# Hybrid stage: V and dt in one product, the relative bias added by VectorE, the decay sums spread by DMA

## The reference, cut to what matters

```python
h = rms_norm(x, mix_norm); proj = h @ w_in             # z 1024 | xbc 1536 | dt 16 | q 512 | k 512 | v 512
xbc = silu(causal_depthwise_conv(xbc, conv_w, conv_b)) # 4 taps; gives xs, B, C
dt = softplus(dt_raw + dt_bias); a = -exp(a_log)
a_cs = cumsum(dt * a)                                  # per head, within a chunk of 128 tokens
y_diag = (C.B) * exp(a_cs[l] - a_cs[s], for s <= l) @ (xs * dt)
y = y_diag + y_off + xs * d_skip;  y = rms_norm(y * silu(z), ssd_norm)
s = q @ k.T * hd**-0.5 + rel_bias[h, qpos - kpos]      # 8 heads of 64; a query chunk of 64 sees its own and earlier ones
att = softmax(s) @ v
out = concat([y, att]) @ w_out
```

## Time and profile before

| what | value |
|---|---|
| median of 3 timed runs | 1182.96 us (1181.51 to 1185.43) |
| span of the profiled execution | 1181.9 us |
| that execution's own timed value | not given apart; the lowest timed run is 1181.51 us |
| TensorE busy | 1162.1 us (98%) |
| VectorE, ScalarE, GpSimd busy | 658.0, 514.1, 51.0 us |
| mean granted TensorE clock | 0.993 |

### The profile page before, as it was taken

The page is one execution under the profiler, slowest core; times in us unless marked ns, Lnnn a source line. Parts: engine busy times, 40 slices in busy tenths (PEclk is TensorE's granted clock), DMA queues, the critical chain, the costliest instruction groups (busy, mean ns, idle before and its releaser), DMA issues.

```text
span 1181.9 us, 18506 instructions
## 1 busy us (share of the span) xinstructions
PE 1162.1 (98%) x7660; PEld 1041.8 (88%) x7668; DVE 658.0 (56%) x717; ACT 514.1 (43%) x581; POOL 51.0 (4%) x93
## 2 busy tenths in 40 slices
PE   9999999999999999999999999999999999999997
PEld 7997999998977799999889999989988878999996
DVE  4757554555654755545654544467854565544543
ACT  4433444443544344444344443445635644434342
POOL 1000000000200100000000000010120010000000
PEclk9999999999999999999999999998989999999999
DMA  9664656554641565565346555556651144456541
GB/s 338 220 211 146 213 178 197 182 180 120 211 161 36 177 219 179 190 183 187 127 144 213 178 177 177 198 156 202 192 164 37 37 161 139 149 181 206 189 148 54
DMA packets 140908, 199.67 MB, mean 169 GB/s; under 512 B 9240, under 2 KB 119024, under 8 KB 140864
## 3 DMA queue, kind: packets, MB, share of 16 engines
q1 hardware_dynamic: 138160, 190.27, 50.0%
q0 software_dynamic: 2704, 8.79, 2.4%
HBM read 197.99 MB, written 1.05 MB: 168 GB/s over the span
## 4 chain that ended last, share of the span: by engine, by line
PE 92%; DVE 3%; ACT 2%; DMA 2%; POOL 1%; issue 1%; SPq 0%; DVEq 0%; POOLq 0%; ACTq 0%
PE up L1401 15%; PE up L1403 15%; PE up L1402 15%; PE acc L1434 11%; PE acc L1435 11%; PE acc L1437 11%; DMA raw<-in_sc_w_in 2%; PE acc L1507 1%; PE up L1489 1%; PE up L1850 1%; PE up L1876 1%; PE up L1478 1%; PE up L1873 1%; PE up L1743 1%; PE up L1423 1%; PE up L1427 1%
## 5 line engine op out<-in xcount | busy, mean ns | idle before, releaser
L933 DVE TENSOR_TENSOR weight_lo<-raw,weight_hi 128x2048 fp32r<-128x2048 f32 (+3 forms) x206 | 414.4, 2017 | 312.4 <-ACT weight_hi L569 312.2
L1401 PE MATMUL up<-xh,weight_hi 128*128 128x256 f32 x1548 | 441.3, 285 | 1.9 <-ACT cols L569 0.8
L569 ACT ACTIVATE weight_hi<-raw 128x2048 fp32r<-128x2048 f32 (+3 forms) x206 | 347.3, 1693 | 213.6 <-PE acc L1437 119.7
L1402 PE MATMUL up<-xl,weight_hi 128*128 128x256 f32 x1548 | 438.9, 283 | 0.0
L1403 PE MATMUL up<-xh,weight_lo 128*128 128x256 f32 x1548 | 438.8, 283 | 0.0
L1401 PEld LDWEIGHTS up<-xh,weight_hi 128*128 128x128 f32 x1548 | 297.8, 192 | 5.9 <-issue 1.7
L1402 PEld LDWEIGHTS up<-xl,weight_hi 128*128 128x128 f32 x1548 | 297.9, 192 | 2.7 <-issue 0.7
L1403 PEld LDWEIGHTS up<-xh,weight_lo 128*128 128x128 f32 x1548 | 297.7, 192 | 0.0
L1434 PE MATMUL acc<-weight_hi,hh 128*128 128x512 f32 x480 | 187.6, 391 | 0.6 <-DVE hl L933 0.4
L1435 PE MATMUL acc<-weight_lo,hh 128*128 128x512 f32 x480 | 187.5, 391 | 0.0
L1437 PE MATMUL acc<-weight_hi,hl 128*128 128x512 f32 x480 | 150.3, 389 | 0.0
(11 more groups left out here) (215 smaller groups left out, 892.7 us busy)
## 6 DMA issues: line engine op xcount, KB each, us to landing
raw<-in_ff_w SPq DMA_DIRECT2D x64, 1024.0 KB, 5.7
raw<-in_ffn_w_gate SPq DMA_DIRECT2D x22, 1024.0 KB, 5.3
raw<-in_ffn_w_up SPq DMA_DIRECT2D x22, 1024.0 KB, 5.4
raw<-in_ffn_w_down SPq DMA_DIRECT2D x44, 512.0 KB, 4.7
raw<-in_w_in SPq DMA_DIRECT2D x16, 1024.0 KB, 5.7
raw<-in_sc_w_in SPq DMA_DIRECT2D x11, 1024.0 KB, 7.3
raw<-in_w_out SPq DMA_DIRECT2D x6, 1024.0 KB, 5.0
raw<-in_sc_w_out SPq DMA_DIRECT2D x4, 1024.0 KB, 5.3
```

The costliest lines, as they stand in the source:

```text
L569: return nc.scalar.activation(dst, src, ACT.Copy, **kw)
L933: return vec.tensor_tensor(dst, whole, high.bitcast(F32), ALU.subtract)
L1401: mm(dst, w_h, xh[:, x_tile + k, :], start=first and k == 0, stop=False)
L1402: mm(dst, w_h, xl[:, x_tile + k, :], start=False, stop=False)
```

## The change

V and dt form one matrix of 528 columns (`VDT`), in three slabs of 3, 3 and 2 of the eight 128-row blocks; `fresh_product` writes each token tile in two pieces of 264 columns. The products for dt alone go. ScalarE copies 264 of the 512 V columns, VectorE 248. ScalarE rounds the third slab and HX between the two tiles' `xh`; VectorE splits these two between the two tiles' `xl`. One fp32 matmul gives the cumulative sums as rows (32 x 128), VectorE copies them to `rows`, GpSimd writes them to HBM, and eight DMAs from GpSimd's queue bring 4 heads each back to all 128 partitions of `tmp_a` or `tmp_b`; the subtraction then works in place in SBUF. The attention bias is added by VectorE: `tensor_tensor_reduce` reads the scores in PSUM and the bias window backwards, adds, writes to `prob_b`, and gives the row maximum. The mask is written by GpSimd into the bias windows. `scores(h)` waits for the row maximum of head h-2 instead of its exponentials.

```diff
@@ SP @@
-            for j in range(2):
+            for j, ks in enumerate(VDT_K):          # range(0, 3), range(3, 6), range(6, 8)
                 place_free(HV + j)
-                load(HV + j, raw3(HV + j, 4, HALF), w[:, 4 * j:4 * j + 4, V0:V0 + HALF])
-            place_free(HDT)
-            load(HDT, raw3(HDT, KD, SSD_HEADS), w[:, :, DT0:DT0 + SSD_HEADS])
+                dst = raw3(HV + j, len(ks), VDT)
+                load(HV + j, dst[:, :, 0:ATT_INNER], w[:, ks[0]:ks[-1] + 1, V0:V0 + ATT_INNER])
+                load(HV + j, dst[:, :, ATT_INNER:], w[:, ks[0]:ks[-1] + 1, DT0:DT0 + SSD_HEADS])
@@ GpSimd @@
+            pool.wait_ge(hy["cum_rows"], 1)
+            pool.dma_start(cum_kept, rows[0:TILES * SSD_HEADS, :]).then_inc(hy["cum_kept"], 16)
...
+            pool.wait_ge(hy["cum_kept"], 16)
+            def wide_sums(n):
+                if n < 2:
+                    pool.wait_ge(hy["y_sum"], SSD_GROUPS)
+                else:
+                    pool.wait_ge(hy["exp"], n - 1)
+                four = cum_kept[4 * n:4 * n + 4, :].rearrange("(a h) l -> a (h l)", a=1).to_broadcast([P, HALF])
+                pool.dma_start((tmp_a, tmp_b)[n % 2][:, :], four).then_inc(hy[f"cum_wide{n % 2}"], 16)
+            pool.wait_ge(hy["hank"], 16 * HEADS)
+            nc.gpsimd.memset(hankel[0:ATTN_CHUNK, :, 0:ATTN_CHUNK], MASKED).then_inc(hy["bias_ready"], 1)
+            for n in range(8):
+                wide_sums(n)
@@ ScalarE @@
-            operand_hi(5, S_HY - 1)
+            operand_hi(5, S_HY - 1, between=True)
-                act.wait_ge(slab_used, HV + 2)
-                copy(v_b[:, tile, :], acc[:, tile, :]).then_inc(hy["v_out"], 1)
+                act.wait_ge(slab_used, HV + 3)
+                copy(v_b[:, tile, 0:VDT // 2], acc[:, 2 * tile, 0:VDT // 2]).then_inc(hy["v_out"], 1)
@@ VectorE @@
+            def biased(h, S):
+                if h >= 2:
+                    dve.wait_ge(att[1]["turned"], h - 1)
+                else:
+                    dve.wait_ge(hy["bias_ready"], 1)
+                for n, (a, b) in enumerate(((0, P), (P, 384))):
+                    ins = vec.tensor_tensor_reduce(prob_b[:, h % 2, a:b], S[:, a:b], hankel[:, h, 0:b - a][:, ::-1], 1.0, MASKED,
+                                                   ALU.add, ALU.max, head_max[:, 0, h, n:n + 1])
+                then(ins)
-            operand_lo(5)
+            operand_lo(5, [0])
             followers(S_HY - 1)
+            operand_lo(5, [1])
+            dve.wait_ge(slab_used, HV + 3)
+            for tile in range(TILES):
+                vec.tensor_copy(v_b[:, tile, VDT // 2:], acc[:, 2 * tile + 1, 0:ATT_INNER - VDT // 2])\
+                    .then_inc(hy["v_out"], 1)
...
+                    vec.tensor_copy(rows[0:TILES * SSD_HEADS, :], acc[0:TILES * SSD_HEADS, 2, P:2 * P])\
+                        .then_inc(hy["cum_rows"], 1)
...
-                    dve.wait_ge(hy["seg_ps"], n + 1)
-                    if n >= 2:
-                        dve.wait_ge(hy["exp"], n - 1)
+                    dve.wait_ge(hy[f"cum_wide{n % 2}"], 16 * (n // 2 + 1))
                     for q in range(4):
-                        vec.tensor_scalar((tmp_a, tmp_b)[n % 2][:, c], up[n % 2][:, c], cum_head(tile, 4 * (n % 4) + q), 0.0,
-                                          ALU.subtract, ALU.min).then_inc(hy["seg"], 1)
+                        row = (tmp_a, tmp_b)[n % 2][:, q * P:(q + 1) * P]
+                        vec.tensor_scalar(row, row, cum_head(tile, 4 * (n % 4) + q), 0.0, ALU.subtract, ALU.min)\
+                            .then_inc(hy["seg"], 1)
@@ TensorE @@
-            fresh_product(5, HV, acc[:, 0, :], HALF, 0, lambda: turn_tile(5, normed, 1))
-            fresh_product(5, HV, acc[:, 1, :], HALF, 1)
-            weights(HDT)
-            token_product(HDT, lambda t: acc[:, 2, t * SSD_HEADS:(t + 1) * SSD_HEADS], SSD_HEADS, SSD_HEADS, KD, 0, True, True)\
-                .then_inc(slab_used, 1)
+            fresh_product(5, HV, VDT_K, [acc[:, n, 0:VDT // 2] for n in (0, 1)], VDT // 2, 0, lambda: turn_tile(5, normed, 1))
+            fresh_product(5, HV, VDT_K, [acc[:, n, 0:VDT // 2] for n in (2, 3)], VDT // 2, 1)
...
+                    pe.wait_ge(hy["v_out"], 2 * TILES)
+                    mm(acc[0:TILES * SSD_HEADS, 2, P:2 * P], dt_work[:, 8, :], tri, start=True, stop=True)
...
-            def decay_sums(n):
...
-                for kt in range(tile + 1):
-                    w0 = (tile - kt) * P
-                    mm(dst[:, kt * P:(kt + 1) * P], hankel[:, h, w0:w0 + P], anti, start=False, stop=False,
-                       skip_group_check=True)
...
-                decay_sums(2 * p)
-                decay_sums(2 * p + 1)
```

More of the change, by code:

```diff
@@ L267, in two_blocks @@
         att = [Sems(f"att{i}", "scores negmax probs normed turned t_out o_ps o_hi o_lo") for i in range(2)]
-        hy = Sems("hy", "rows tap0 conv xbc dt_abs dt_exp adt qk_out v_out cum_ps cum_out decays xs_ps xs_out y_skip xdt "
-                        "hank cb_ps cb_act cb seg_ps seg exp seg_w y_ps off_ps off_taken y_sum z_gate y_gated sumsq "
-                        "rstd y_n y_ps_t y_hi y_lo")
+        hy = Sems("hy", "rows tap0 conv xbc dt_abs dt_exp adt qk_out v_out cum_ps cum_out cum_rows cum_kept cum_wide0 cum_wide1 decays "
+                        "xs_ps xs_out y_skip xdt hank bias_ready cb_ps cb_act cb seg exp seg_w y_ps off_ps off_taken "
+                        "y_sum z_gate y_gated sumsq rstd y_n y_ps_t y_hi y_lo")
         def up_view(w):
@@ L1246, in _ @@
             vec.tensor_tensor(neg_abs, neg_abs, x_dt, ALU.min).then_inc(hy["dt_abs"], 1)
[L1247 removed]
+            split_slab(HV + 2 + RING)
             dve.wait_ge(hy["dt_exp"], 2)
@@ L1608, in token_product, with fresh_product, pieces @@
                 return ins
-            def fresh_product(b, m, dst, n, tile, middle=lambda: None):
+            def fresh_product(b, m, k_tiles, dst, n, tile, middle=lambda: None):
                 open_group = dict(skip_group_check=True)
-                blocks = [(j, 4 * j + k, slice(k * n, (k + 1) * n)) for j in range(2) for k in range(4)]
                 cut = slice(tile * P, (tile + 1) * P)
[L1616 to L1621, removed]
-                middle()
[L1623 to L1627, removed]
+                def pieces(j, f):
+                    at = (f - k_tiles[j][0]) * n * len(dst)
+                    return [(d, slice(at + i * n, at + (i + 1) * n)) for i, d in enumerate(dst)]
+                for j, ks in enumerate(k_tiles):
+                    weights(m + j)
+                    for f in ks:
+                        if f % 4 == 0:
+                            pe.wait_ge(operand_high, 4 * b + 2 * tile + f // 4 + 1)
+                        for d, c in pieces(j, f):
+                            mm(d, xh[:, f, cut], weight_hi[:, (m + j) % RING, c], start=f == 0, stop=False, **open_group)
+                            mm(d, xh[:, f, cut], weight_lo[:, (m + j) % RING, c], start=False, stop=False, **open_group)
+                middle()
+                for j, ks in enumerate(k_tiles):
+                    for f in ks:
+                        if f % 4 == 0:
+                            pe.wait_ge(operand_low, 4 * b + 2 * tile + f // 4 + 1)
+                        for d, c in pieces(j, f):
+                            ins = mm(d, xl[:, f, cut], weight_hi[:, (m + j) % RING, c], start=False, stop=f == KD - 1,
+                                     **open_group)
+                    if tile:
@@ L1628, in fresh_product @@
                         ins.then_inc(slab_used, 1)
+            BY_FOUR = (range(0, 4), range(4, KD))
             def key_latent(j, tile):
@@ L1692, in _, with attention @@
             ins.then_inc(slab_used, 1)
-            def attention(i, score, prob, v, s_bank, t_bank, o_dst, o_banks):
+            def attention(i, score, scores_read, per_head_read, prob, v, s_bank, t_bank, o_dst, o_banks):
                 q = att[i]
@@ L1743, in mla_score @@
                 mm(dst, q_rot[r, h // 2, queries], k_rot[r, keys], start=False, stop=False, skip_group_check=True)
+                return mm(dst[:, tile * P + P - ATTN_CHUNK:tile * P + P], mask_row[:, :], mask_ones[:, :], start=False,
+                          stop=True, skip_group_check=True)
             def latent_rows(c):
@@ L1838, in _ @@
             keys_queries(3)
-            def decay_sums(n):
-                tile, h0 = n // 4, 4 * (n % 4)
-                bank = up[n % 2]
-                if n >= 2:
-                    pe.wait_ge(hy["seg"], 4 * (n - 1))
-                else:
-                    pe.wait_ge(hy["off_taken"], n + 1)
-                for q in range(4):
-                    ins = mm(bank[:, q * P:(q + 1) * P], adt_tile(tile)[:, h0 + q:h0 + q + 1].to_broadcast([P, P]),
-                             tri, start=True, stop=True)
-                ins.then_inc(hy["seg_ps"], 1)
             def scan_outputs(n):
```

57 lines of the change are left out of this document (28 added, 29 removed).

## The result

The changed kernel takes 1165.23 us (median of 4 runs, 1164.75 to 1165.52) against 1183.51 us (4 runs of the kernel before beside it): a ratio of 0.9845, 95% interval 0.9831 to 0.9859. The prediction was 1167.5 with a range of 1161.5 to 1175.5. The profiled spans are 1181.9 and 1162.9 us, 19.0 apart, where the sum of the prediction had 15.2. Within one kernel the shorter executions are those with the higher mean granted clock (the kernel before, beside the first experiments: 1180.3 us at 0.994 and 1184.8 us at 0.990), so one profile shows one draw of the clock.

What follows compares the result with a forecast made beforehand. TensorE, busy 98% of the span, was taken as the bound. Terms -0.2 - 21.2 + 0.9 + 0.3 + 5.0 = -15.2 us took the span from 1181.9 to 1166.7; forecast 1167.5 us, range 1161.5 to 1175.5.

Steps and rivals of the forecast that it cites:

- -21.2 + 0.9 + 0.3: Scores to w_out: 21.2 us saved with half clock, 0.9 lost waiting for normalised odd heads, 0.3 for dearer reduces.
- Part 1: V and dt product up to the transposes: TensorE gains 5.0 us but keeps 0.2, VectorE's chain being late.
- TensorE is 5.0 ahead. VectorE is not.: At the start of xbc: TensorE gains 5.0 us, while VectorE's next slab split comes 3.3 us later.
- Part 3: Clock falls behind new TensorE gaps of 2.9 us at 790.5 and 5 us at 844.2: 5.0 us lost in all.
- The second fall: Half clock behind the 5 us gap at 844.2, over transposes, q and k: nothing to 3.4 us, 2.5 taken.
- The rival without falls: Both new TensorE gaps are short enough to keep full clock: -20.2 us, 1162.7 us; chance 0.2.
- Part 2: Scores and decay sums: removed matmuls save 17.8 us at full clock, 21.2 with the half clock in 871 to 888.
- the sign of being right: At the w_out product: it would start 14 to 17 us earlier, one of several signs listed.
- The half clock in the scores: In 871 to 888: 6.8 us at half clock cost 3.4 us, expected to go with the removed matmuls.
- About 9 us ahead: Decay-sum broadcasts after pass 0 are issued about 9 us early, following an exponential of the pass before, so hidden.
- The loop rival: Decay-sum broadcasts and exponentials wait on each other; the gain is gone at 14.2 us landing time; chance 0.03.
- the second rival: The attention part loses its clock or waits more, for broadcasts or dearer reduces: 1171 to 1178 us; chance 0.2.

Runs made afterwards that it cites:

- the first experiments: The earliest follow-up runs, starting with only the V/dt product changed against the kernel before: 1185.5 us against 1184.08.
- its repetition: The changed kernel run again with nothing altered, beside the gap-filling run: 1166.21 us, ratio 0.9839 to the kernel before.
- the filled gap: The changed kernel with 17 useless matmuls ahead of TensorE's wait for the decays: 1164.65 us, ratio 0.9834 to the kernel before.
- The V/dt kernel: The kernel before with only the V/dt product changed; bias, mask and decay sums stay matmuls: 1185.5 us, ratio 1.0004.

## Why the prediction was right, and where it was off

Cut at the same marks, the prediction and the profiled execution compare so:

| stretch | predicted | measured |
|---|---|---|
| up to the transposes | -0.2, and +2.5 for a fall of the clock | -0.6 (-1.3, and V 0.7 later) |
| transposes to scores | +2.5 for a fall | +2.7 |
| scores to w_out | -21.2 + 0.9 + 0.3 = -20.0 | -21.1 |
| sum | -15.2 | -19.0 |

**Part 1 was right in mechanism.** The third slab was late (2.1 us for 2.9: ScalarE and VectorE had it ready at 793.5, as I said, but TensorE started 0.7 later). xbc began at 803.21, predicted 803.2; VectorE's split at 805.91, predicted 806.0; the transposes waited 4.0, predicted 5, and ran at 848.90, predicted 849.3. The two runs that take part 1 away or keep it alone show no gain from it. "TensorE is 5.0 ahead. VectorE is not." was the right step. VectorE's chain starts with the V copies, which wait for TensorE's last V/dt matmul (idle 6.28), so a gap in V/dt goes through to the end in full, as I had reckoned and as splitting the third slab first showed: xbc to transposes is 45.69 us in the changed kernel (803.21 to 848.90), in its repetition (804.74 to 850.43) and in that variant (800.23 to 845.92). What I had not seen is that the last 3.2 us of the wait (the last conv and its silu ahead of the exponential) were an order of work: nothing in them fed the decays.

**Part 3 was mis-sized, and it is the largest error.** "I take 2.5 for both: 5.0." The second fall cost 2.5, 2.4 and 1.6 in the three executions of the changed kernel, by the filled gap's 23.12. The first did not come in the profiled execution, and when it comes it costs 1.6: the mean clock of 0.72 over 6 us in the repetition is 3.4 us at half clock, where I had reckoned with up to 6.8. So the term was 2.5 in the first profile, about 4 in the second and 1.6 in the third, for 5.0: whether the first fall comes and what the second costs differ from one execution to the next. The rival without falls was half right, in one place of two.

**Part 2, scores: too small by 2.3 us.** I took the bias and mask matmuls out of the row of starts (0.55 + 0.77 = 1.32 a head) and left the q.k matmuls at their price between them, 1.04. They cost 0.85 a head when nothing stands between them, and 0.43 a head for the first two, which run together. Gross 12.9 for 10.6. The waits for VectorE took 1.6 where I had 0.9 (0.66, 0.30, 0.37 and 0.26 us). The reduce cost about 0.1 us more than the maximum each, within my 0.3 in all for TensorE's end. Decay sums: 7.2 gross, 5.9 to 6.2 net by the run that puts them back. A pass was to take 12.2 us and 0.3 of waits, and took 12.2 with its waits in it; the w_out product came 19.0 earlier, outside the 14 to 17 that I had named as the sign of being right.

**The half clock in the scores came right by luck, as far as the runs show.** I had put 3.4 us on it because "the work that stood in them is mostly what goes". The V/dt kernel keeps all of that work, and its clock is at 1.00 there, with 3.0 us less from the scores on (77.47 for 80.50). So 3.0 of the 19.0 between the two profiles are not shown to come from the change. Without them part 2 is worth 18.0 (77.47 - 59.43), where the prediction had 17.8 - 1.2 = 16.6.

**The broadcasts were hidden, but not by as much as I said.** They landed after 3.5 and 3.7 us (medians of four) where I took 4.5. "About 9 us ahead" holds for the last two pairs only: the first pair was issued 5.4 us ahead of its subtraction (873.80 for 879.17), the second 5.6. GpSimd's and VectorE's timelines at the second pair:

```profile
881.10 0.54 POOL L563 DMA_DIRECT2D tmp_a<-cum_kept  x1 [6.24 <-ACT tmp_c L909]
```

```profile
886.70 0.87 DVE L1383 TENSOR_SCALAR tmp_a<-tmp_a,arena 128x128 f32<-128x128 f32 x4
```

The loop rival needed 14.2. (Its last figures were off: by its own formula a landing time of 16 us gives 10 + 17.1 - 20.2 = +6.9 and, with falls, 1195, not +5 and 1193.) I had set a statement of the page "SBUF — State Buffer" of the Trainium skill (SBUF: two separate sides) against this, by which the forecast would have been 1168.5: no broadcast here shows such a delay. But none had the occasion: the subtractions ran in 879.2 to 880.8, 886.7 to 888.4, 902.0 to 903.7 and 914.2 to 915.8, and each broadcast was issued and had landed between two of these stretches (issues at 873.8 to 874.9, 881.1 to 882.3, 890.5 to 891.6 and 903.9 to 905.2). So the rule itself is not tested, and at a landing time of 7 us the first two pairs would have come late.

**The attention part kept its clock,** at 1.00 in every stretch from 875 to 930, against the second rival, though TensorE now has four small waits in it.

## What to carry to other kernels

When an engine at 98% gets a lead in one part, look at which list is to hand it the next operand: here TensorE's 5 us were lost behind one exponential that stood behind a silu for no reason of data, and moving it gave 5.8 us, more than TensorE's whole lead. A gap of 2 to 4 us in TensorE can be dearer than its length: where the clock fell behind it, by 1.6 to 2.5 us of half clock in the changed kernel's executions. So a change that makes a gap should be priced with a range for it. Price what stays as well as what goes: matmuls that become neighbours can cost less than they did apart.

## What the hardware showed that I had not expected

- Two heads' q.k matmuls, with 64 rows each in opposite halves, took 0.86 us together when adjacent, 1.99 with one full-height matmul between them (that matmul included), and one head alone 0.85. The kernel scores one head per step, so six heads pay 0.85; scoring them in pairs was not tried.
- The same 2.1 us gap was followed by half clock in six recorded executions of eight. Behind the 4 us gap it came in all seven, at a price of 1.6 us in one execution and 2.4 or 2.5 in two others of the same kernel. One profile does not tell what a gap costs.
- `tensor_tensor_reduce` with a second operand read backwards, from PSUM, took 0.42 us for 256 elements and 0.29 for 128, and the read of its result 0.08: as a plain maximum of the same width (0.41) but for the read.
